# Expert gathers by slot for 128 tokens, and the V sum in 64x64 blocks

## The reference

```python
def one_block(hb):
    q = (hb @ w_query).reshape(t, PEER_HEADS, 2, PEER_HALF)
    s = jnp.einsum('thpc,phkc->thpk', q, keys)
    ...                                   # top 16 of 128 twice, then of 256
    idx = jnp.take_along_axis(cand_idx, top_pos, axis=-1).reshape(t, 128)
    gate = jax.nn.softmax(top_s, axis=-1).reshape(t, 128)
    u = expert_u[idx]
    act = jax.nn.gelu(jnp.einsum('tnd,td->tn', u, hb))
    return jnp.einsum('tn,tnd->td', gate * act, expert_v[idx])
```

## Time and profile before

| | |
|---|---|
| runs | 3843.14 us median of 3 (3839.8 to 3851.57) |
| span of the profiled execution | 3673.8 us (its own time is not given on the page) |
| TensorE busy, share of the span | 3377.1 us, 92% |
| DVE busy | 2002.4 us, 55% |
| GpSimd busy | 1994.0 us, 54% |
| ScalarE busy | 604.3 us, 16% |
| DMA moved | 1147.96 MB, of it 1090.65 MB by the software queue of the gathers |
| mean granted TensorE clock | 0.976 |

### The profile page before, as it was taken

The page is one execution under the profiler, slowest core; times in us unless marked ns, Lnnn a source line. Parts: engine busy times, 40 slices in busy tenths (PEclk is TensorE's granted clock), DMA queues, the critical chain, the costliest instruction groups (busy, mean ns, idle before and its releaser), DMA issues.

```text
span 3673.8 us, 38389 instructions
## 1 busy us (share of the span) xinstructions
PE 3377.1 (92%) x8894; PEld 1243.9 (34%) x8894; DVE 2002.4 (55%) x5133; ACT 604.3 (16%) x1621; POOL 1994.0 (54%) x2137
## 2 busy tenths in 40 slices
PE   7999968999999999988999999998999999999998
PEld 3664322332233223323333333323332333322223
DVE  1032565765566656653577457655666556744441
ACT  1044101111111111111111111111111111111111
POOL 0001025656655665555666656666566655666774
PEclk9999977999999999998999999999999999999999
DMA  2121048989998999999999989999999998999997
GB/s 92 69 103 52 1 150 327 334 318 387 386 327 323 396 390 334 329 386 348 354 344 340 392 326 349 338 388 347 328 344 383 358 331 320 368 389 375 400 400 271
DMA packets 326594, 1147.96 MB, mean 312 GB/s; under 512 B 38080, under 2 KB 43200, under 8 KB 324416
## 3 DMA queue, kind: packets, MB, share of 16 engines
q0 software_dynamic: 299520, 1090.65, 79.8%
q1 hardware_dynamic: 26944, 55.92, 4.3%
HBM read 1137.88 MB, written 8.49 MB: 312 GB/s over the span
## 4 chain that ended last, share of the span: by engine, by line
PE 65%; DMA 21%; issue 7%; DVE 4%; ACT 2%; POOL 1%; SPq 0%; ACTq 0%; DVEq 0%; POOLq 0%
PE psum L1290 37%; DMA v_ring<-in_peer_v,idx_v 19%; PE psum L1283 8%; PE psum L936 6%; PE psum L518 3%; PE psum L612 2%; PE psum L638 2%; DVE u_ring L1366 2%; DMA u_ring<-in_peer_u,idx_u 1%; PE psum L549 1%; ACT w_col L1329 1%; PE psum L1021 1%; PE psum L968 1%; PE psum L581 1%; PE psum L542 1%
## 5 line engine op out<-in xcount | busy, mean ns | idle before, releaser
L1290 PE MATMUL psum<-v_ring,w_col 128*128 128x512 f32 x4160 | 2083.4, 624 | 183.5 <-DMA v_ring<-in_peer_v,idx_v 126.7
L1366 DVE SCALAR_TENSOR_TENSOR u_ring<-u_ring,psum 128x1024 f32<-128x1024 f32 x1040 | 1267.3, 1220 | 1242.2 <-PE psum L1283 1174.4
L1261 POOL DMA_INDIRECT u_ring<-in_peer_u,idx_u x1040 | 985.4, 947 | 949.9 <-PE psum L1290 431.4
L1265 POOL DMA_INDIRECT v_ring<-in_peer_v,idx_v x1040 | 987.5, 950 | 376.7 <-issue 170.7
L1290 PEld LDWEIGHTS psum<-v_ring,w_col 128*128 128x128 f32 x4160 | 711.6, 190 | 1182.7 <-issue 774.6
L1283 PE MATMUL psum<-hparts,pick 48*128 48x512 bf16 x2080 | 644.8, 391 | 50.5 <-DVE u_ring L1366 34.4
L1329 ACT ACTIVATE w_col<-strip,weight 128x128 f32<-128x128 f32 (+1 forms) x1040 | 398.5, 399 | 1651.9 <-PE psum L1290 1650.7
L1283 PEld LDWEIGHTS psum<-hparts,pick 48*128 48x128 bf16 x2080 | 116.1, 95 | 790.9 <-DVE u_ring L1366 470.0
L936 PE MATMUL psum<-wq,hbT 128*128 (+1 forms) x512 | 259.4, 602 | 1.2 <-ACT hbT L893 1.2
L451 POOL IOTA iota<- 128x16 f32 x1 | 0.1, 145 | 336.5 <-ACT catT L718 336.5
L936 PEld LDWEIGHTS psum<-wq,hbT 128*128 128x128 f32 x512 | 98.9, 194 | 125.4 <-issue 124.0
(11 more groups left out here) (220 smaller groups left out, 1531.9 us busy)
## 6 DMA issues: line engine op xcount, KB each, us to landing
u_ring<-in_peer_u,idx_u POOLq DMA_INDIRECT x1040, 6.1
v_ring<-in_peer_v,idx_v POOLq DMA_INDIRECT x1040, 6.1
wq<-in_peer_w_query SPq DMA_DIRECT2D x16, 1024.0 KB, 14.1
w_ring<-in_even_w_in SPq DMA_DIRECT2D x6, 2048.0 KB, 8.1
hparts<-parts_dram SPq DMA_DIRECT2D x65, 96.0 KB, 5.4
parts_dram<-part SPq DMA_DIRECT2D x24, 256.0 KB
w_ring<-in_even_w_out SPq DMA_DIRECT2D x1, 4096.0 KB, 14.0
hres<-in_x SPq DMA_DIRECT2D x4, 512.0 KB, 5.3
```

Source lines behind the costliest of these rows:

```text
L1261: nc.gpsimd.indirect_dma_start(u_ring[:, i % U_SLOTS, :], None, u_rows, bass.IndirectOffsetOnAxis(idx_u[par][:, i:i + 1], 0)).then_inc(s_u ...
L1265: nc.gpsimd.indirect_dma_start(v_ring[:, i % V_SLOTS, :], None, v_rows, bass.IndirectOffsetOnAxis(idx_v[par][:, i:i + 1], 0)).then_inc(s_v ...
L1290: ins = nc.tensor.matmul(y_ps[:, half, :], w_col[:, i % W_SLOTS, :], v_ring[:, i % V_SLOTS, 512 * half:512 * half + 512], start=False, sto ...
L1366: nc.vector.scalar_tensor_tensor(out=row, in0=row, scalar=1.0, in1=bc[i % 2].rearrange("p a b -> p (a b)"), op0=ALU.mult, op1=ALU.mult, ac ...
```

## The change

The gathers are turned. A partition now stands for a token of the tile, and a gather fetches for 128 tokens at once the row of their n-th expert: slot n. There are still 128 gathers of u and 128 of v for a tile, of the same size. The tables are used as they come out of the routing, so `tail_tensor` goes. The dot of a slot multiplies `u_ring` with the tile's normed rows themselves, kept in SBUF in `hd` (`keep_scalar` copies them, two tiles deep), so `pick`, `hparts`, the splitting, `save_parts`, `fetch_parts` and the broadcast matmuls go. The V sum of a slot multiplies each token's row by its own weight: `w_col` becomes the diagonal of the weights, 64 columns wide for each half of the partitions. Two slots e = 0, 1 are taken together: row half r of slot e goes to column half (r + e) % 2 of the output, into bank 2r + half. So each half of 512 columns takes four matmuls of 64x64 by 64x512 on the four quarters of the array. Four banks stay open instead of two, and `take_sum` puts the halves together. The meta chunk keeps its old form, with groups of experts folded (`fold`, `spread`, `sel`). Nothing changes in `gather_pool` or in the number of slots of the rings.

```diff
-        def experts_tensor(pe, u, v, par, fetched, hooks=()):
-
-            if u is not None:
-                pe.wait_ge(s_fetched[par], 16 * fetched)
-            for i in range(CHUNK):
-                if u is not None:
-                    wait(pe, s_dot, CHUNK * u + i - 1)
-                    for half in range(2):
-                        ins = nc.tensor.matmul(bc[i % 2][:, half, :], pick[:, i, :],
-                                               hparts[:, par, 512 * half:512 * half + 512], start=True, stop=True)
-                    ins.then_inc(s_bc, 1)
-                if v is not None:
-                    pe.wait_ge(s_v[i % V_SLOTS], 16 * ((CHUNK // V_SLOTS) * v + i // V_SLOTS + 1))
-                    pe.wait_ge(s_wcol, CHUNK * v + i + 1)
-                    for half in range(2):
-                        ins = nc.tensor.matmul(y_ps[:, half, :], w_col[:, i % W_SLOTS, :],
-                                               v_ring[:, i % V_SLOTS, 512 * half:512 * half + 512],
-                                               start=False, stop=False, skip_group_check=True)
-                    ins.then_inc(s_acc, 1)
+        def experts_tensor(pe, v, hooks=()):
+
+            for i in range(0, CHUNK, 2):
+                at_token(hooks, i - 1)
                 at_token(hooks, i)
+                for e in range(2):
+                    pe.wait_ge(s_v[(i + e) % V_SLOTS], 16 * ((CHUNK // V_SLOTS) * v + (i + e) // V_SLOTS + 1))
+                pe.wait_ge(s_wcol, CHUNK * v + i + 2)
+                apart(pe)
+                for half in range(2):
+                    for e in range(2):
+                        for r in range(2):
+                            rows, to = slice(64 * r, 64 * r + 64), (r + e) % 2
+                            ins = nc.tensor.matmul(y_bank(r, half)[64 * to:64 * to + 64, :], w_col[rows, (i + e) % W_SLOTS, 0:P // 2],
+                                                   v_ring[rows, (i + e) % V_SLOTS, 512 * half:512 * half + 512],
+                                                   start=False, stop=False, skip_group_check=True)
+                        if half:
+                            ins.then_inc(s_acc, 1)
+            at_token(hooks, CHUNK - 1)
...
-        def dots_vector(dve, u, par, hooks=(), first=False):
+        def dots_vector(dve, u, par, rows, hooks=(), first=False):
...
-                dve.wait_ge(s_bc, CHUNK * u + i + 1)
                 row = u_ring[:, i % U_SLOTS, :]
-                nc.vector.scalar_tensor_tensor(out=row, in0=row, scalar=1.0, in1=bc[i % 2].rearrange("p a b -> p (a b)"),
+                nc.vector.scalar_tensor_tensor(out=row, in0=row, scalar=1.0, in1=rows,
                                                op0=ALU.mult, op1=ALU.mult, accum_out=dot[par][:, i:i + 1]).then_inc(s_dot, 1)
...
-        def take_sum(dve, tiles, dst, n):
+        def take_sum(dve, tiles, dst):
             dve.wait_ge(s_y, tiles + 1)
-            nc.vector.tensor_tensor(dst, dst, y_ps[0:n, :, :].rearrange("p a b -> p (a b)"), ALU.add).then_inc(s_yadd, 1)
+            for r in range(2):
+                rows, other = slice(64 * r, 64 * r + 64), slice(64 - 64 * r, 128 - 64 * r)
+                nc.vector.tensor_copy(y_other[rows, :], psum[other, 2 * r:2 * r + 2, :].rearrange("p a b -> p (a b)")).then_inc(s_ystep, 1)
+                nc.vector.tensor_tensor(dst(r), dst(r), psum[rows, 2 * r:2 * r + 2, :].rearrange("p a b -> p (a b)"),
+                                        ALU.add).then_inc(s_ystep, 1)
+            dve.wait_ge(s_ystep, 4 * tiles)
+            nc.vector.tensor_tensor(dst(), dst(), y_other[:, :], ALU.add).then_inc(s_yadd, 1)
             dve.wait_ge(s_yadd, tiles + 1)
...
+        def keep_scalar(act, job, dotted):
+
+            act.wait_ge(s_hb, job + 1)
+            if dotted is not None:
+                act.wait_ge(s_dot, dotted)
+            apart(act)
...
+            half = job % 2
+            dst = hd[:, bass.ds(half, 1), :].rearrange("p a d -> p (a d)")
+            nc.scalar.copy(dst, hb[:, :]).then_inc(s_hd, 1)
```

More of the change, by code:

```diff
@@ L154, in program @@
         hbT = sb("hbT", [P, KD, P])
-        part = [sb(f"part{i}", [P, D], BF16) for i in range(PARTS)]
-        pick = sb("pick", [PARTS * CHUNK, CHUNK, P], BF16)
+        squares = sb("squares", [P, D], BF16)
+        hd = sb("hd", [P, 2, D])
+        meta_hf = sb("meta_hf", [META, D])
         ffn_g = sb("ffn_g", [P, D])
@@ L249, in program @@
         s_hbT = sem("hbT_copied")
[L250 to L253, removed]
+        s_hd = sem("hb_kept_for_dots")
         s_q_ps = sem("query_multiplied")
@@ L397, in program @@
         ODD_LOADS = 6 * 16
[L399 to L411, removed]
         def mixer_constants(pool):
@@ L904, in norm_vector, with hb_free @@
             dve.wait_ge(s_hb, job + 1)
[L906 to L915, removed]
+        def hb_free(dve, job):
+            wait(dve, s_hbT_ps, job)
+            wait(dve, s_hd, job)
+            apart(dve)
+        def keep_scalar(act, job, dotted):
[3 more added lines that the diff above has]
+            apart(act)
+            if isinstance(job, int) and job == 0:
+                nc.scalar.copy(meta_hf[:, :], hb[0:META, :]).then_inc(s_hd, 1)
+                return
+            half = job % 2
+            dst = hd[:, bass.ds(half, 1), :].rearrange("p a d -> p (a d)")
+            nc.scalar.copy(dst, hb[:, :]).then_inc(s_hd, 1)
         def start_tensor(pe, job, n, layer):
@@ L1299, in open_sum @@
             pe.wait_ge(s_setup, SETUP_STEPS)
-            for half in range(2):
-                nc.tensor.matmul(y_ps[:, half, :], zeros[:, 0:P], zeros[:, :], start=True, stop=False, skip_group_check=True)
+            for bank in range(4):
+                nc.tensor.matmul(psum[:, bank, :], zeros[:, 0:P], zeros[:, :], start=True, stop=False, skip_group_check=True)
         def close_sum(pe):
-            for half in range(2):
-                ins = nc.tensor.matmul(y_ps[:, half, :], zeros[:, 0:P], zeros[:, :], start=False, stop=True, skip_group_check=True)
+            for bank in range(4):
+                ins = nc.tensor.matmul(psum[:, bank, :], zeros[:, 0:P], zeros[:, :], start=False, stop=True, skip_group_check=True)
             ins.then_inc(s_y, 1)
@@ L1382, in program, with rows_for @@
         QUERY_BANK = psum[:, 4, :]
+        def rows_for(half):
+            return hd[:, bass.ds(half, 1), :].rearrange("p a d -> p (a d)")
         def halves(hooks):
@@ L1623, in _ @@
             add_projected(dve, 3)
-            for i in range(SPLIT + 1):
-                split_vector(dve, 0, META, i)
             norm_vector(dve, 1, P, tile_of(0), 0)
@@ L1629, in _ @@
             logits_vector(dve, 0, P, 2)
-            for i in range(SPLIT + 1):
-                split_vector(dve, 1, P, i)
             gates_vector(dve, 0, P, 2)
@@ L1648, in _, with pair @@
                 add_projected(dve, i)
-            def pair(j, s, first=(), second=()):
+            def pair(j, s, rows, first=(), second=()):
                 u = TILE_CHUNKS * j + 3 + 2 * s
-                dots_vector(dve, u, 1, first)
-                dots_vector(dve, u + 1, 0, second)
+                dots_vector(dve, u, 1, rows, first)
+                dots_vector(dve, u + 1, 0, rows, second)
             def iteration(j, layer, start=()):
```

240 lines of the change are left out of this document (119 added, 121 removed).

## The result

| | before | after |
|---|---|---|
| median of the runs | 3843.03 us (3839.8 to 3851.57) | 4459.56 us (4453.94 to 4470.98) |
| ratio | 1 | 1.1623, 95% interval 1.1582 to 1.1664 |
| span of the profiled execution | 3673.8 us | 4452.2 us (its own time 4453.94) |
| mean granted TensorE clock | 0.976 | 0.731 |

The change costs 617 us by the runs and 778 us by the two spans. The forecast was 4430 us. The time was right, but by luck: two errors of nearly equal size cancelled in it.

What follows compares the result with a forecast made beforehand. The closed four-slot V ring was taken to set the pace: +548 us for slots, +14 tail, +30 tile sums and -6 start took the 3673.8 us span to 4260; with 169.3 added, forecast 4430 us, range 3880 to 4800.

Steps and rivals of the forecast that it cites:

- The handshake by pairs closes the ring: Four-slot V ring: both slots return only near a pair's end, so GpSimd refills after it; round 13.54 us at full clock.
- Time of the pair: TensorE's eight block matmuls, 16 records, for two V slots: bounded between 2.0 and 7.15 us, taken as 4.1.
- the chain: Likeliest case, chance 0.47: block matmuls start strictly in order, nine steps, 4.1 us a pair; range 4250 to 4650 us.
- my first rival: Block matmuls run four at a time on TensorE, pair 2.0 us, 3.75 at low clock; 4175 us, chance 0.24.
- Clock: TensorE idles 2.7 of 6.8 us a pair; a fifth of all slots at the low clock, 3.54 us a slot.
- Flight: Gather's time from issue to landing in the V ring: taken as 5.4 us, between 5.3 thin and 6.1 dense.
- Blocked issues: GpSimd gather issues delayed by the DVE dot with two SBUF inputs: 0.1 us each, 0.4 us a round.
- Sum of a tile: On DVE one addition becomes four half-height operations and one addition, delaying TensorE's next tile: +30 us for eight tiles.
- Start: First dot waits only for its u rows, not the broadcast through DRAM: between 0 and -10 us, taken as -6.
- The ring's total: V ring's 1008 slots at 3.54 instead of 2.996 us: +548 us; tail of 32 V sums: +14 us.
- The constant of 169.3 us: Difference between profiled span and median of the runs, taken as constant and added to the 4260 us span: 4429 us.
- The rival "faster": Pair round falls below the old one, deciding at 11.98 us, if the gathers' flight is short; 3700 us, chance 0.13.

Runs made afterwards that it cites:

- e1_slot: Changed kernel with V sums taken one slot at a time instead of by pairs, same 64x64 matmuls: 3684.87 us beside 3675.48 for the kernel before, ratio 1.0015.
- e1_warm: Changed kernel with 16 bf16 matmuls of zeros behind each pair, in TensorE's idle time: 4270.17 us, ratio 1.1611 to the kernel before.
- e2_order: Changed kernel with a pair's eight block matmuls reordered, the two column halves innermost: 4460.21 us beside 4458.83 for the changed kernel.
- e3_pairps: Changed kernel, pairs kept, with VectorE copying the tile's rows into PSUM for the dot: 4345.48 us, ratio 1.1818 to the kernel before.
- e2_diagps: As e2_diag, but the tile's rows for the dot are kept in PSUM instead of SBUF: 3731.68 us, ratio 0.9667 to the kernel before.
- e0_before: The kernel before, unchanged, as a control with a profile: 3677.86 us with a span of 3672.2 us.
- e3_before: The kernel before, unchanged, profiled again in another set: 3680.34 us with a span of 3678.3 us.
- e2_diag: Changed kernel with full 128x128 diagonals, two matmuls a slot, slot by slot, one addition a tile: 3723.81 us, ratio 0.9657 to the kernel before.

## Why the prediction was right, step by step

**The handshake by pairs closes the ring: right.** It was the central step, and e1_slot shows it alone: without the pairs the loss is gone. The form of the round, its four issues and the wait for TensorE, stood as drawn. Of its terms several were off. In the table the forecast round of 14.16 us becomes 15.1 by +0.4 in the issues (the first two steps together), +0.7 in the flight, +0.6 from landing to sum, and -0.7 in the sum.

**Time of the pair: wrong.** I took the chain, 4.1 us. It is 1.95 us at the full clock (e1_warm; 1.97 in e2_order) and 3.69 at the low one (3472.07 above). The price of my first rival, 2.0 and 3.75, was right, and the starts in fours are its sign. So the case that I held for likeliest, the chain at 0.47, did not happen; the rival at 0.24 did, and its own forecast was 4175. I had let a reading of an order of starts decide where no row did. The Trainium skill (TensorE: Matmul & The Clock Gate, Part 3: Packing small matmuls) has matmuls of separate tiles overlap but start and end in program order; the overlap is in this trace (16 records in 1.95 us), the order of starts is not borne out by e2_order (1.97 us, where I had estimated 4.5).

**Clock: right in kind, far off in size.** I put a fifth of the slots at the low level; 380 of the 512 pairs had a mean granted clock below 0.75. TensorE's 4.97 us of idleness before the pair shown above are longer than the gap of 1.96 us in the earlier trace rows. And I had expected query work in half of the gaps; it stands right before 145 of the 512 pairs. Of these 73 ran below 0.75, of the other 367 it was 307. The two errors pulled against each other: the sum, predicted at 3.86 us with its clock, measured 3.13.

**Flight: too short.** I took 5.4 us with nothing behind it; issue to landing measured 6.10, and 0.58 follow until the sum starts. The median of the earlier trace rows, 6.1, was the right row, also for thinner traffic; the earlier trace rows are V gathers alone. The reaction from landing to sum had no term at all. These two put 1.3 us more into the round than I had.

**Blocked issues: right.** 0.4 us a round in the forecast; the mean issue is 1.08 us against 0.94, which for four is 0.56, and e3_pairps took 105 us back by them. The order of time has the same picture as the earlier trace rows:

```profile
3811.53 1.23 DVE L1377 SCALAR_TENSOR_TENSOR u_ring<-u_ring,hd 128x1024 f32<-128x1024 f32 x1 [4.27 <-DMA u_ring<-in_peer_u,idx_u]
3812.10 1.47 POOL L1263 DMA_INDIRECT u_ring<-in_peer_u,idx_u  x1 [0.30 <-issue]
```

The issue begins 0.57 us into the dot and ends 0.81 us after it (3813.57 against 3812.76). Over the whole trace after, 715 of the 2080 issues begin inside such a dot; they take 1.34 us on average and end 0.81 us (median) after it. An issue that is already under way when a dot begins keeps its 0.94 us (506 such issues, 0.94 on average). The Trainium skill (SBUF — State Buffer, Who interferes with whom) has the rule that a VectorE instruction with two SBUF inputs contends with a GpSimd instruction that reads SBUF. e2_diagps agrees with it: with one of the two inputs in PSUM the issues take 0.943 and 0.939 us again. That it is a read by which the issue is held no run shows.

**Sum of a tile: right.** +30 us predicted. TensorE's wait at `open_sum` is 44.3 us, where it was 11.3:

```profile
PE psum L1313 <- DVE hres L1397: 44.3, 7, 6.3
```

**Start: small.** -6 predicted; the first sum of the tiles starts 12.5 us earlier (617.5 against 630.0).

**The ring's total: too low.** From the first to the last of the 1024 V sums 3818.5 us pass, and before 3033.1: +785, of which 33 are the tiles' sums. I had 548 + 14 + 30 = 592. The span came out at 4452 and not at 4260; what does it is the round, 15.1 us for 14.2.

**The constant of 169.3 us: wrong, and it hid the last error.** I added it as time around the span. By e0_before and e3_before time around the span is 2 us; the rest is the difference between the quick execution that I read and the runs of another kind, and the kernel after has no such difference. 4260 and 2 us would have been my honest 4262, 190 to 200 us too low; with 169 more it came to 4430. Both lie inside the range of 3880 to 4800, so the direction and the range held without luck, and only the closeness of 4430 is owed to it. A span that differs from the timed runs by 4% where nothing explains it should have widened the doubt, not been added.

**The rival "faster"** had its point of decision at a round of 11.98 us. e1_slot has one of 12.0 and is level with the kernel before: the limit was in the right place. A slip in another rival: by the formula of the forecast's tail, the tail without sharing is 32 us and not 25, which moves 4835 by 7.

## What to carry to other kernels

Where a ring of buffers is closed, write its round as a sum of steps: whatever must come together before a slot is given back (two landings, a burst of issues) adds its full spread to the round, and a cheaper sum cannot pay for that. Ask first what the ring's depth is worth: e2_diagps took 3732 us, and with four slots more 3325, on another chip, while taking 364 us of blocked issues off GpSimd in e2_diag had moved nothing. And compare the span of the trace that you read with the timed runs; where they differ by more than a few microseconds and nothing in the trace explains it, they may come from executions on different chips.

## What the runs showed of the hardware

64x64 f32 matmuls on the four quarters of the array, into separate banks or halves of banks, run at the same time: eight of them take 1.95 us at the full clock, 0.43 us a record as for one of 128x128, in either of the two orders of issue that were run. Two quarters at a time take 1.93 us a slot (e1_slot, median), as much as two full 128x128 matmuls (1.95 in e2_diag).

A gather's issue on GpSimd that begins during a dot with both inputs in SBUF ends 0.81 us after the dot; one that begins before the dot, or during a dot with one input in PSUM, takes 0.94 us (989 issues in the kernel before begin so).

The kernel before took 3675 and 3680 us on two chips and 3843 and 3864 us in the two other sets of runs, the kernel after 4450 to 4460 in all three of its sets. A ratio between two kernels can differ by 5% between chips, here from 1.155 to 1.210.
